# Norms between layers: sums of squares inside the last projection, factors spread by products with the identity

## The reference, cut

```python
def rms_norm(x, g):
    xf = x.astype(jnp.float32)
    y = xf * lax.rsqrt(jnp.mean(xf * xf, axis=-1, keepdims=True) + EPS)
    return (y * g.astype(jnp.float32)).astype(x.dtype)

def modulate(x, g, shift, scale):
    return rms_norm(x, g) * (1 + scale[:, None]) + shift[:, None]

def swiglu(h, w13, w2):
    a, b = jnp.split(h @ w13, 2, axis=-1)
    return (jax.nn.silu(a) * b) @ w2

# first block, for each of 2 layers
mod = c_act @ ada_w[l] + ada_b[l]
sh1, sc1, g1, sh2, sc2, g2, sh3, sc3, g3 = jnp.split(mod, N_ADA, axis=-1)
h = modulate(x, norm_g[l, 0], sh1, sc1)
x = x + 0.5 * g1[:, None] * swiglu(h, ff_w13[l, 0], ff_w2[l, 0])
h = modulate(x, norm_g[l, 1], sh2, sc2)
# y: hybrid of convolution and attention in layer 0, NSA attention in layer 1, both of h
x = x + g2[:, None] * y
h = modulate(x, norm_g[l, 2], sh3, sc3)
x = x + 0.5 * g3[:, None] * swiglu(h, ff_w13[l, 1], ff_w2[l, 1])
# then rms_norm(x, final_g); second block: forget attention with memory attention, SwiGLU,
# conformer convolution with memory attention, mixture of 8 experts; third block: MoBA attention
# with pooling, cross attention, convolutional feed-forward
```

## Time and profile before

| | us |
|---|---|
| median of 3 runs | 3522.67 |
| lowest and highest | 3520.62, 3531.55 |
| profiled execution | 3529.03 |
| its span | 3527.1 |
| PE busy | 3266.1 (93%) |
| DVE busy | 2303.5 (65%) |
| ACT busy | 1682.8 (48%) |
| mean granted TensorE clock | 0.924 of full |

### The profile page before, as it was taken

One profiled execution on the slowest core, in us unless ns is written; L12 is line 12 of the kernel. 1 busy time (PEld: TensorE's weight loads), 2 busy tenths in 40 slices (PEclk: granted clock), 3 DMA queues, 4 the chain that ended last, 5 costly groups with the idle time before them and its releaser, 6 DMA issues.

```text
span 3527.1 us, 49487 instructions
## 1 busy us (share of the span) xinstructions
PE 3266.1 (93%) x21234; PEld 2958.7 (84%) x21234; DVE 2303.5 (65%) x2627; ACT 1682.8 (48%) x1860; POOL 84.8 (2%) x164
## 2 busy tenths in 40 slices
PE   6998999999999999999717999999999999989999
PEld 6998899999879998899617877778778778889899
DVE  6776677676445553444583878778778778644575
ACT  4434343434424343343303767667667667535453
POOL 1010001010000000000000000000000000000000
PEclk9998899999978998899856999999999999989999
DMA  7784367586313542145301879779779789522252
GB/s 268 264 291 175 132 237 286 211 285 224 126 36 123 207 155 84 60 184 187 108 0 49 317 296 367 293 300 363 302 301 364 302 304 361 215 96 108 108 187 113
DMA packets 112379, 739.67 MB, mean 210 GB/s; under 512 B 12500, under 2 KB 12500, under 8 KB 32128
## 3 DMA queue, kind: packets, MB, share of 16 engines
q1 hardware_dynamic: 89424, 651.21, 49.2%
q0 software_dynamic: 22704, 84.91, 6.7%
HBM read 735.02 MB, written 1.05 MB: 209 GB/s over the span
## 4 chain that ended last, share of the span: by engine, by line
PE 79%; DVE 6%; ACT 2%; issue 1%; DMA 0%; DVEq 0%; ACTq 0%; POOLq 0%
PE ps L482 63%; PE ps L481 14%; DVE AF L2431 3%; PE ps L491 2%; DVE wlo L2449 1%; ACT whi L1644 1%; DVE X L2422 0%; DVE hl L2422 0%; DVE AR L3323 0%; DVE T L2422 0%; ACT hh L1632 0%; ACT rT L1632 0%; DVE X L2431 0%; DVE AR L2428 0%; DVE gf L2434 0%
## 5 line engine op out<-in xcount | busy, mean ns | idle before, releaser
L2449 DVE TENSOR_TENSOR wlo<-ring,whi 128x2048 fp32r<-128x2048 f32 x620 | 1419.4, 2291 | 547.5 <-ACT whi L1644 546.8
L1644 ACT ACTIVATE whi<-ring 128x2048 fp32r<-128x2048 f32 x620 | 1184.8, 1913 | 347.2 <-issue 223.4
L482 PE MATMUL ps<-whi,AR 128*128 128x512 f32 (+1 forms) x2724 | 879.6, 398 | 0.0
L482 PE MATMUL ps<-hh,whi 128*128 128x256 f32 x2752 | 790.3, 287 | 0.8 <-DVE hl L2431 0.8
L482 PE MATMUL ps<-hl,whi 128*128 128x256 f32 x2752 | 783.7, 285 | 0.0
L482 PE MATMUL ps<-hh,wlo 128*128 128x256 f32 x2752 | 783.3, 285 | 0.0
L482 PEld LDWEIGHTS ps<-whi,AR 128*128 128x128 f32 x2724 | 511.4, 188 | 118.5 <-issue 1.6
L482 PE MATMUL ps<-wlo,AR 128*128 128x512 f32 (+1 forms) x1362 | 536.9, 394 | 0.0
L482 PEld LDWEIGHTS ps<-hh,whi 128*128 128x128 f32 x2752 | 532.8, 194 | 2.3 <-issue 2.0
L482 PEld LDWEIGHTS ps<-hl,whi 128*128 128x128 f32 x2752 | 532.6, 194 | 0.2
L482 PEld LDWEIGHTS ps<-hh,wlo 128*128 128x128 f32 x2752 | 531.8, 193 | 0.2
(11 more groups left out here) (200 smaller groups left out, 3440.5 us busy)
## 6 DMA issues: line engine op xcount, KB each, us to landing
ring<-in_w SPq DMA_DIRECT2D x620, 1024.0 KB, 4.9
rring<-in_r POOLq DMA_DIRECT2D x151, 512.0 KB, 5.0
AF<-in_mem POOLq DMA_DIRECT2D x2, 1024.0 KB, 5.9
X<-in_x POOLq DMA_DIRECT2D x1, 1024.0 KB, 12.9
AF<-in_cst POOLq DMA_DIRECT2D x1, 1024.0 KB, 5.2
y_out<-X SPq DMA_DIRECT2D x1, 1024.0 KB, 3.9
cst<-in_cst POOLq DMA_DIRECT2D x1, 606.0 KB, 4.5
sm<-in_small POOLq DMA_DIRECT2D x1, 378.0 KB, 4.8
```

The lines of the kernel that those rows point to most:

```text
L482: return self.e.matmul(out, l, r, start=start, stop=stop)
L1644: self.e.activation(N.whi[:, c % HB, :], N.ring[:, c % RING, :], ACT.Copy).then_inc(N.sem["hi"], 1)
L2449: self.e.tensor_tensor(N.wlo[:, c % HB, :], N.ring[:, c % RING, :], N.whi[:, c % HB, :].bitcast(F32), ALU.subtract).then_inc(N.sem["lo"], 1)
```

## The change

- **Spread.** `spread` takes the place of `rows_of`, `rows_out` and `bcast` wherever one factor per token is wanted: two fp32 products, each with the column of `st` repeated 128 times as weights and the identity as what is streamed. ACT's copy is gone. `st` has four rows, and `root` now waits for `stfree`, the spread four rows earlier. Head norms keep the old way.
- **Sums inside.** For the nine pairs in `NEXT`, the sums of tiles 0 and 1 stand in the last chunk of the projection before, behind column block 5, those of tiles 2 to 7 behind its block 7. The four warm-ups between the sums are gone in every norm, and the 18 behind the spread are 12. ACT squares tiles 6 and 7 singly, and runs a root of one column ahead of the squares, so that the table is loaded there.
- **In turn.** DVE scales a tile and makes the lower half of the tile two places before it in turn. PE's first products go tile by tile over both column blocks (`fresh`), in `ffn` over both first chunks at once (`wide`).
- **`ada_sums`** of a step stand behind the next step's last chunk; on DVE those of the last step stand behind `finish`.
- **`cv`.** In `conv_layer` ACT makes the norm's squares ahead of its wait for everything, not behind it.

```diff
+NEXT = {("ff", 0, 0): "hy", "hyout": (("ff", 0, 1), "n"), ("ff", 0, 1): (("ff", 1, 0), "n"), ("ff", 1, 0): "nsa",
+        "nsaout": (("ff", 1, 1), "n"), ("ff", 1, 1): "final", "foxout": "n_ffn2", "ff2": "cv", "x3out": "n_ffn3"}
...
-    def stat(self, key, tiles, inds=None, heat=0):
+    def stat(self, key, tiles, inds=None):
+
         n = len(tiles)
         self.take_row(key)
-        b = self.take((key, "ss"))
-        for k in range(n):
-            if k == n // 2 and heat:
-                self.heat(heat)
+        self.take((key, "ss"))
+        self.stat_part(key, tiles, range(n), inds)
+
+    def stat_part(self, key, tiles, part, inds=None):
+        n, b = len(tiles), self.ps((key, "ss"))
+        for k in part:
             self.wait_ge("act", (key, "sq", k))
             for tb in range(2):
                 l = tiles[k][:, tb * P:(tb + 1) * P]
@@ -544,25 +557,31 @@
                 else:
                     o = tb * 2 * n + 2 * k
                     i = self.mm(b[:, o:o + 2], l, inds, True, True)
-        i.then_inc(*self.up((key, "ss")))
+        if part[-1] == n - 1:
+            i.then_inc(*self.up((key, "ss")))
+
+    def spread(self, key, bank=None, ready=("dve", "rstd")):
+
+        st = self.N.st[:, self.row[key] % 4, :]
+        b = self.take((key, "bc"), bank)
+        self.wait_ge(ready[0], (key, ready[1]))
+        for tb in range(2):
+            t = self.mm(b[:, tb * P:(tb + 1) * P], st[:, tb:tb + 1].to_broadcast([P, P]), self.N.ident, True, True)
+        t.then_inc(*self.up((key, "bc"), ("stfree", self.row[key])))
 
     def rows_of(self, key, G):
         st = self.N.st[:, self.row[key] % 4, :]
         b = self.take((key, "rows"))
         self.wait_ge("dve", (key, "rstd"))
         self.tr(b[0:G, 0:P], st[:, 0:G])
-        self.tr(b[0:G, P:S], st[:, G:2 * G]).then_inc(*self.up((key, "rows")))
-
-    def rinv(self, key, tiles, G=None):
-        self.stat(key, tiles, self.N.C("half") if G else None)
-        self.rows_of(key, G or 1)
-
-    def bcast(self, key, lhs, name="bc", last=True, bank=None):
-        b = self.take((key, name), bank)
+        self.tr(b[0:G, P:S], st[:, G:2 * G]).then_inc(*self.up((key, "rows"), ("stfree", self.row[key])))
...
-        self.factors(key, [T[:, k, :] for k in range(n)])
-        self.heat(9)
-
-    def factors(self, key, tiles, heat=2, bank=None):
-
-        self.stat(key, tiles, heat=heat)
-        self.rows_of(key, 1)
-        self.bcast(key, self.N.ones[0:1, :], bank=bank)
...
+    def wide(self, keys, specs, h):
+
+        N = self.N
+        cs = [self.chunk(s) for s in specs]
+        bs = [self.take(k) for k in keys]
+        for k in range(8):
+            self.ready(h, k)
+            for key, (i, whi, wlo), b in zip(keys, cs, bs):
+                for j in range(2):
+                    o = k * S + j * P
+                    t = self.mm3(b[:, j * S:(j + 1) * S], whi[:, o:o + P], wlo[:, o:o + P], N.hh[:, k, :], N.hl[:, k, :],
+                                 k == 0 and j == 0, k == 7, skip=True)
+                if k == 7:
+                    t.then_inc(*self.up(key, ("chunk", i)))
...
+        if self.fresh == h:
+            self.fresh = None
+            for k in range(nk):
+                self.ready(h, k)
+                for j in range(nj):
+                    o = off + k * wid + j * P
+                    t = self.mm3(b[:, j * S:(j + 1) * S], whi[:, o:o + P], wlo[:, o:o + P], hh[:, k, :], hl[:, k, :],
+                                 k == 0 and j == 0, k == nk - 1, skip=True)
+            t.then_inc(*self.up(key))
+            self.chunk_done()
+            for j in range(nj):
+                yield
+            return
...
+            if f == nf - 1 and j == 5 and key in NEXT:
+                self.take_row(NEXT[key])
+                self.take((NEXT[key], "ss"))
+                self.stat_part(NEXT[key], tiles, (0, 1))
             if j in cuts:
                 yield
         self.chunk_done()
+        if f == nf - 1 and key in NEXT:
+            self.stat_part(NEXT[key], tiles, range(2, 8))
...
-        for f in range(2):
-            up_a(f)
-            up_b(f)
+        self.wide([(key, "a", 0), (key, "b", 0)], [ga(0), gb(0)], h)
+        self.fresh = None
+        up_a(1)
+        up_b(1)
+        last = ()
...
-            for g in groups:
+            for g in last:
                 self.ada_sums(g)
+            last = groups
...
+        if n == 8:
+            if self.loaded:
+                self.wait_ge("act", self.loaded)
+            self.act(self.N.misc[:, 62:63], self.N.C("eps"), ACT.Sqrt)
+            self.loaded = self.here()
+        for k in (0, 2, 4, 6, 7) if n == 8 else range(0, n, 2):
+            m = min(2, n - k) if k < 6 else 1
...
+        if self.row[key] >= 4:
+            self.wait_ge("mm", ("stfree", self.row[key] - 4))
...
-        self.rinv(key, n * P)
+        self.root(key, n * P)
...
+        self.norm("cv", N.X, ("V", "norm_mix_2", 1))
         self.wait_ge("mm", f)
         self.wait_ge("dve", f)
         self.wait_ge("act", f)
-        self.norm("cv", N.X, ("V", "norm_mix_2", 1))
...
-        self.scaled_rows(key, N.T, X, gain, n, lambda k: (key, "n", k))
-        self.lower(key, N.T, N.hl, N.hh, n, shift)
+        self.wait_ge("mm", (key, "bc"))
+        b = self.ps((key, "bc"))[:, 0:S]
+        for k in range(n + 2):
+            if k < n:
+                self.stt(N.T[:, k, :], X[:, k, :], gain[:, k:k + 1], b, ALU.mult, ALU.mult, (key, "n", k),
+                         *([("free", (key, "bc"))] if k == n - 1 else []))
+            if k >= 2:
+                self.lower(key, N.T, N.hl, N.hh, (k - 2,), shift)
...
+            if f < NF - 1:
+                for g in last:
+                    self.ada_sums(g)
+                last = groups
         if coef:
             self.need_mod(*coef)
         self.finish(key, coef)
+        for g in last:
+            self.ada_sums(g)
```

101 lines of the change are left out of this document (41 added, 60 removed).

## The result

| | before | after |
|---|---|---|
| median of the runs | 3521.64 us (3513.81 to 3531.55) | 3484.80 us (3480.19 to 3494.38) |
| ratio of after to before | | 0.9897, 95% interval 0.9865 to 0.993 |
| profiled execution, its span | 3529.03, 3527.1 us | 3480.19, 3478.4 us |
| mean granted clock of that execution | 0.924 | 0.932 |

The change makes the kernel 37 us faster at the median; 20.5 were forecast (3502, range 3483 to 3518). The two profiled executions are 48.8 apart, more than the medians: the one of before was among the longest of its runs, the one of after the shortest. What sets such differences, and why it matters for every comparison here, comes out under the experiments.

What follows compares the result with a forecast made beforehand. TensorE bounds the kernel, with 79% of the chain that ended last. Terms of -16.5 - 8.8 - 8.7 + 8.5 + 6.6 - 3.3 + 4.2 - 2.5 sum to -20.5 us, giving 3502; range 3483 to 3518.

Steps and rivals of the forecast that it cites:

- rival 1: Norms: the pause is short enough that the clock mostly stays up, so the kernel reaches 3479; chance 12%.
- term of the clock: Six norms with sums inside the chunk: sums falling behind the clock's drop cost 0.2 more each; +6.6 us (0 to +14).
- term of the six warm-ups: End of the norms: 12 warm-ups for 18 start the layer earlier, partly lost to low clock; -8.7 us (-16 to 0).
- rivals 3 and 4: 3: sums all low, shorter warm-up gains nothing, 3518, 7%; 4: pause inside the chunk drops clock at once, 3539, 5%.
- Spreading: From root to scaling: identity products save 1.1 us in each of 15 places, -16.5; the other spreads, -2.5.
- Rival 2: Spreading: the identity product costs what four transposes cost, so that term is 0 and the kernel takes 3519; chance 8%.
- Warm-ups: Norms: four fewer amid the sums, -8.8 us, and six fewer at the end, -8.7 us.
- Sums inside the chunk: Last chunk before six norms: PE stands 1.7 us at block 5 for squares, less old waits of 0.8; +8.5 us.
- `cv`: Norm `cv`: squares ahead of the wait for all of X remove 2.18 us of waiting and speed the sums; -3.3 us.
- `hy`: Norm `hy`: PE stands some 6 us at block 5, ending at low clock; scaling at 303, now 300.48; +4.2 us.
- The table of the root: Norms: loading the root table ahead of the squares changes nothing, since it was hidden under the sums; 0.
- theory of luck: Whole kernel, stated for the experiments: the surplus gain is only where the clock's falls happen to lie; no chance given.

Runs made afterwards that it cites:

- e9: Kernel before with only the spreading by two identity products added, everything else as before: 3499.4 us, ratio 0.9935.
- e3: Changed kernel with four warm-ups amid the sums and eighteen behind the spreading put back in all 13 norms: 3490.5 us, ratio 0.9913.
- e7: Changed kernel without any of the twelve warm-ups behind the spreading: 3502.3 us, ratio 0.9947.
- e10: Changed kernel with only the four warm-ups amid the sums put back in 13 norms: 3493.0 us, ratio 0.9908.
- e2: Changed kernel with all eight tiles' sums behind the last chunk, none amid it: 3476.5 us, ratio 0.988.
- e4: Changed kernel with the sums of each `ada` group behind their own chunk again, not one chunk later: 3491.5 us, ratio 0.9913.
- e5: Changed kernel without the early load of the root's table, which is loaded behind the squares again: 3480.9 us, ratio 0.9903.
- e6: Changed kernel with all eight tiles scaled before the first lower half and the layer's old start; twelve warm-ups stay: 3502.1 us, ratio 0.995.
- e1: Changed kernel with the old spreading (transposes, copy by ACT, product with the ones) back in 15 places on the path: 3508.3 us, ratio 0.9966.

## Why the prediction was right, and where it was not

The direction, the mechanism of the largest term and the range held. The size did not: 20.5 were booked, 37 came (35.1 by the means, over all runs). The range held by 1.8 us (3484.8, lower end 3483), less than the median is sure to, so that it held is in part luck. The number of rival 1 (3479) lies nearer to the result than the forecast's 3502.

- **The step that failed is the term of the clock.** I booked +6.6 for it (ends 0 and +14). Measured, the mean clock rose from 0.9265 to 0.9298, which by the 2.5 us per 0.001 is 8 us less, not 6.6 more. At equal clock the change is worth 27.0 us; my sum without the clock term is 27.1. That the two agree so closely is in part luck, since terms inside it were off both ways, and the term of the six warm-ups had a loss of clock in it too (8.7 for a length of 16). Rival 1 (3479, 12%) had the sign right: in the norm of `("ff",1,0)` the clock stayed at 1.00 through all sixteen sums. It was not so everywhere: in `("ff",0,1)` and `n_ffn3` it fell right behind the pause at block 5, and the twelve sums took 5.1 us (rivals 3 and 4 below). What I missed was to ask, of each part that goes, whether PE's thin stretch gets shorter; I asked it only of the part that comes.
- **Spreading**, 19.0 booked with the other places: 20.1 (e9). Up to what is behind it the pair of products takes 0.88 at half clock or 0.47 at full, where 1.15 was booked; reciprocal to scaling is 1.48 where it was 2.52. Rival 2 is out.
- **Warm-ups**, 17.5 booked for both kinds: 13.1 at equal clock, 5.7 in time (e3). I had them as cost only, with half of the six at the end written off to the clock; those behind the spreading hold it up, and with none of these the kernel loses 17 (e7). Those amid the sums show no gain of clock (e10).
- **Sums inside the chunk**, +8.5 booked for the pause: +8.3 (e2, for the whole part: with the clock term I had booked more, about 13 by my own sum for e2). Of the waits booked at 1.7, `("ff",0,1)`, `cv` and `n_ffn3` show 1.57, 1.62 and 1.45, and `("ff",1,0)`, `nsa` and `final` 0.85, 0.85 and 0.76, since deferred sums fill the rest (e4 shows 1.69). `("ff",1,1)` and `n_ffn2` pay nothing, as said.
- **`cv`**, -3.3 booked: from the chunk to the first product 9.1 us instead of 16.3. No wait of 2.18 any more. More than booked, since this norm got the clock as well: its twelve sums took 2.73, where sixteen had taken 3.06 and 3.41 with warm-ups between.
- **`hy`**, +4.2 booked. The wait came as forecast, 6.61 for about 6, and scaling started at 300.65 for 300.48, no earlier, as said. But 303 was too late by 2.3, so that the term came to about +1.9. The rows, with their windows, tell why:

```profile
290.78 1.84 PE L489 MATMUL ps<-ones,T 128*128 128x1 f32 x8 [6.61 <-ACT T L1673]
...
295.19 2.86 PE L489 MATMUL ps<-ones,T 128*128 128x1 f32 x24
```

```profile
288.60:295.40 6.80, 4.62 (x22) 4.65 (x23) 2.88 (x7) 1.89 (x3) 0.00 (x0) 0.50 0.83 295
295.40:298.90 3.50, 3.50 (x31) 3.45 (x31) 0.88 (x2) 1.07 (x3) 0.00 (x0) 0.99 0.01 2
```

The clock fell in the wait, but came back at 295.4 behind twelve dense products, and the twelve sums took 2.86 for the 5.2 booked at half clock.
- **The table of the root**, 0 booked: +3.9 by e5, 1.4 each at `moe` and `moba` by the rows.
- **The start tile by tile**, 0 booked and rightly so as long as it goes together with the shorter warm-up: without it PE waits 1.93 behind the twelve warm-ups, and the kernel is 17.3 us slower, 10.5 at equal clock (e6).
- **Rivals 3 and 4** (low clock over the start; the pause drops the clock at once) did not come as totals: at `("ff",1,0)` the window over the pause shows 1.00, and at `cv` a pause of 1.62 left it up through all the sums. But their mechanism was there at two of the six places with a pause. At `("ff",0,1)` (pause 1.57) the clock fell 0.3 us after the pause ended, and the twelve products of blocks 6 and 7 took 2.7 us where they take 1.4 at full clock:

```profile
436.51:439.22 2.71, 2.71 (x14) 2.71 (x14) 0.00 (x0) 0.06 (x1) 0.00 (x0) 0.50 0.42 172
```

At `n_ffn3` (pause 1.45) it fell 1.4 us after the pause, and these products took 2.4. In both norms chunk to layer is longer than before, 13.6 for 11.1 and 12.6 for 12.1 us. Why a pause of 1.62 left the clock up and one of 1.45 did not, no run here shows. The Trainium skill (TensorE: Matmul & The Clock Gate, "HAM oscillation — how this bites in real kernels") tells of waits for DMA between bursts, longer than these pauses, behind which each burst starts at the low clock. The trace agrees for the long wait: the 6.61 at `hy` brought the clock down.

The theory of luck is neither true nor out: executions of one program differ by as much as a part is worth, and of the 66 us of half clock that the profiled execution of after has less, 32 lie outside the norms. But over its runs the changed kernel's clock is 0.9298, not 0.932, so a good part of these 32 belongs to that one execution. The 34 in the norms go with norms that are 24.8 us shorter, and e1, with the spreading undone, has 18 of them back.

## What to carry to other kernels

A relay between engines (reciprocal, transpose, copy, product) is worth cutting by a hop: a product of a broadcast column with the identity does what a transpose, a copy and a product with the ones did, 20 us over 28 places. Here the new step was less work on the bounding engine too (27.2 us for 41.6); whether a hop pays where it is more, no run shows. On an engine whose clock depends on its load, price every edit twice, its own length and what it does to the thin stretches around it; filler was cost where it delayed the work (e10: 8.2 us, no gain of clock) and gain where it filled a wait (e7). And compare such kernels with the granted clock of each run beside its time, since it explains most of what two runs of one program differ by.
